# Router of an expert-retrieval layer: query weights as the stationary operand, score matmuls one expert tile later, weight rows of 8 KB

## What is computed

```python
q = (xn @ wq).reshape(B, S, PEER_HEADS, 2, PEER_HALF)          # 8 heads, 2 halves of 128
s1 = einsum('bshd,nd->bshn', q[..., 0, :], k1)                 # 128 keys each
s2 = einsum('bshd,nd->bshn', q[..., 1, :], k2)
t1, i1 = top_k(s1, 16);  t2, i2 = top_k(s2, 16)
top_s, pos = top_k(t1[..., :, None] + t2[..., None, :], 16)    # of 256 candidates
gate = softmax(top_s);  idx = i1 * 128 + i2 at pos             # 16 of 16384 experts
act = gelu(einsum('td,ted->te', x_blk, u[i_blk]))              # rows of 2048 from table u
out = einsum('te,ted->td', g_blk * act, v[i_blk])              # rows of 2048 from table v
```

## Time and profile before

| | |
|---|---|
| median of 3 runs | 3597.04 us (3596.82 to 3602.62) |
| span of the profiled execution | 3600.9 us |
| PE, DVE, POOL, ACT busy | 82%, 51%, 52%, 15% of the span |
| mean granted TensorE clock | 0.907 of full speed |
| HBM read | 1225.74 MB, 341 GB/s over the span |

### The profile page before, as it was taken

The page is one execution under the profiler, slowest core; times in us unless marked ns, Lnnn a source line. Parts: engine busy times, 40 slices in busy tenths (PEclk is TensorE's granted clock), DMA queues, the critical chain, the costliest instruction groups (busy, mean ns, idle before and its releaser), DMA issues.

```text
span 3600.9 us, 28564 instructions
## 1 busy us (share of the span) xinstructions
PE 2935.1 (82%) x8424; PEld 1628.0 (45%) x8424; DVE 1833.3 (51%) x3313; ACT 548.9 (15%) x1123; POOL 1857.2 (52%) x1173
## 2 busy tenths in 40 slices
PE   7999977888878877788779797888888877777777
PEld 6876743444444333333337685444444433333333
DVE  2021145555555566656557833555555555566564
ACT  3344210000000100000023341000000000000001
POOL 4767634444444555555537644454544444545553
PEclk9999989998999888888989898999999988888899
DMA  5544579999998999999975336999999899999998
GB/s 205 175 145 147 179 284 382 376 383 385 375 385 350 420 420 421 420 421 421 420 324 187 105 117 241 377 383 386 385 387 384 363 420 420 421 421 420 420 421 352
DMA packets 240791, 1228.63 MB, mean 341 GB/s; under 512 B 21088, under 2 KB 54624, under 8 KB 108512
## 3 DMA queue, kind: packets, MB, share of 16 engines
q0 software_dynamic: 147456, 1073.81, 72.6%
q1 hardware_dynamic: 92560, 148.67, 12.4%
q10 hardware_dynamic: 720, 5.44, 0.4%
HBM read 1225.74 MB, written 2.10 MB: 341 GB/s over the span
## 4 chain that ended last, share of the span: by engine, by line
PE 29%; DMA 29%; issue 19%; POOL 12%; DVE 9%; ACT 2%; POOLq 0%; DVEq 0%; ACTq 0%; SPq 0%
DMA ring_sb<-in_peer_u_dram,idx_cur 28%; PE bank L908 21%; POOL w_parts L322 8%; PE bank L788 6%; POOL ring_sb L442 3%; DVE ring_sb L1208 2%; POOL ring_sb L433 1%; PE bank L742 1%; DVE arena L1294 1%; DVE arena L1301 1%; ACT diag L606 1%; DVE arena L1302 1%; PE bank L803 0%; DVE shared L1063 0%; DVE shared L1059 0%
## 5 line engine op out<-in xcount | busy, mean ns | idle before, releaser
L908 PE MATMUL bank<-ring_sb,diag 128*128 128x512 f32 x4096 | 1954.6, 640 | 522.9 <-ACT diag L606 522.9
L1208 DVE CUSTOM_DVE_ANT_0 ring_sb<-ring_sb,arena 128x2048 f32<-128x2048 f32 x512 | 1169.4, 2293 | 928.4 <-DMA ring_sb<-in_peer_u_dram,idx_cur 927.8
L908 PEld LDWEIGHTS bank<-ring_sb,diag 128*128 128x128 f32 x4096 | 833.1, 206 | 1635.6 <-issue 1444.4
L442 POOL DMA_INDIRECT ring_sb<-in_peer_v_dram,idx_cur x512 | 690.8, 1349 | 740.2 <-PE bank L908 570.5
L433 POOL DMA_INDIRECT ring_sb<-in_peer_u_dram,idx_cur x512 | 651.8, 1273 | 604.5 <-DVE shared L1208 430.9
L322 POOL TENSOR_TENSOR w_parts<-ring_sb,w_parts 128x2048 fp32r<-128x2048 f32 x98 | 457.9, 4684 | 240.4 <-ACT w_parts L316 240.4
L742 PE MATMUL bank<-w_parts,actT_hi 128*128 128x512 f32 x1664 | 527.8, 399 | 24.9 <-POOL w_parts L322 12.1
L742 PEld LDWEIGHTS bank<-w_parts,actT_hi 128*128 128x128 f32 x1664 | 319.2, 193 | 97.9 <-POOL w_parts L322 15.4
L742 PE MATMUL bank<-w_parts,actT_lo 128*128 128x512 f32 x832 | 330.0, 397 | 0.0
L601 ACT ACTIVATE shared<-shared 128x4 f32<-128x4 f32 (+1 forms) x140 | 28.8, 206 | 1517.2 <-DVE shared L1217 1517.2
L316 ACT CAST w_parts<-ring_sb 128x2048 fp32r<-128x2048 f32 x104 | 198.2, 1910 | 358.3 <-DMA ring_sb<-in_mlstm_w_in_dram 167.3
(11 more groups left out here) (158 smaller groups left out, 1204.1 us busy)
## 6 DMA issues: line engine op xcount, KB each, us to landing
ring_sb<-in_mlstm_w_in_dram SPq DMA_DIRECT2D x48, 1024.0 KB, 5.1
arena<-in_peer_wq_dram SPq DMA_DIRECT2D x28, 1024.0 KB, 11.1
ring_sb<-in_attn_w_in_dram SPq DMA_DIRECT2D x24, 1024.0 KB, 5.2
ring_sb<-in_mlstm_w_out_dram SPq DMA_DIRECT2D x16, 1024.0 KB, 5.1
ring_sb<-in_attn_w_out_dram SPq DMA_DIRECT2D x16, 1024.0 KB, 5.1
ring_sb<-in_peer_u_dram,idx_cur POOLq DMA_INDIRECT x512, 15.3
ring_sb<-in_peer_v_dram,idx_cur POOLq DMA_INDIRECT x512, 14.0
ring_sb<-in_peer_wq_dram SPq DMA_DIRECT2D x4, 1024.0 KB, 8.9
```

The costliest lines, as they stand in the source:

```text
L442: nc.gpsimd.indirect_dma_start(out=v_slot[k % NVS], out_offset=None, in_=v_rows, in_offset=bass.IndirectOffsetOnAxis(ap=idx_cur[par][:, k: ...
L908: last = mm(acc[n][:, :], diag[k % 4][:, :], v_slot[k % NVS][:, n * CH:(n + 1) * CH], start=False, stop=end and k == TOPK - 1, skip_group_ ...
L1208: v.tensor_tensor_reduce(u_slot[k % NU], u_slot[k % NU], xn[b], 1.0, 0.0, ALU.mult, ALU.add, dots[:, k:k + 1]).then_inc(u_used, 1)
```

## The change

Four edits. The query matmuls take a 128 x 128 piece of the query weights as the stationary operand and the tokens as the moving one, so that the result is the transposed query; the transposes, one of the copies and the tile `q_nat` are gone. The router is split in two on PE and ACT: on PE the query matmuls stay ahead of tile 4 and the score matmuls come ahead of tile 5; on ACT the copy of the query comes behind the diagonals of tiles 4 to 7 and the copy of the scores ahead of the third tanh, with the exponentials of the gates (`gate_exp`) behind it. The host lays out the query weights so that a head's 16 pieces are one row of 16 KB per partition, of which each transfer takes 8 KB; before, a row was 1 KB. For the first head and block 1 the score matmuls also come behind the four matmuls of `seed`.

```diff
 # SP
-                    for i in range(2):
-                        sp.dma_start(slots[i], wq[l, i * half:(i + 1) * half, bass.ds(h * (2 * P), 2 * P)]
-                                     .rearrange("(k p) n -> p k n", p=P)).then_inc(landed[i], 16)
+                    for i in range(2):
+                        sp.dma_start(slots[i].rearrange("p k n -> p (k n)"),
+                                     rows[bass.ds(h * P + l * HEADS * P, P), i * SLOT:(i + 1) * SLOT]).then_inc(landed[i], 16)
 # ACT
-                    act.wait_ge(rq_full, n + 1)
-                    nc.scalar.copy(q_nat[:, lo * 2 * P:hi * 2 * P], mis[0][:, lo * 2 * P:hi * 2 * P]).then_inc(rq_out, 1)
-                    act.wait_ge(rt_full, n + 1)
-                    q_t = [t.rearrange("p (s t) -> p s t", s=2)[:, :, lo * P:hi * P] for t in (q_T[:, :], trb[0][:, :])]
-                    nc.scalar.copy(*q_t).then_inc(rt_out, 1)
+                    q_t = [t.rearrange("p (s t) -> p s t", s=2)[:, :, lo * P:hi * P] for t in (q_T[:, :], mis[0][:, :])]
+                    nc.scalar.copy(*q_t).then_inc(rq_out, 1)
+
+                def router_scores(h, blocks=slice(0, NB)):
...
                     for j, (k0, k1) in enumerate(groups):
-                        if j == 1 and head is not None:
-                            router(head)
+                        if j == 2 and head is not None:
+                            router_scores(head)
+                        if j == 2 and more:
+                            gate_exp(gu + 1)
...
-                        if j == 1 and more:
-                            gate_exp(gu + 1)
+                        if j == 1 and head is not None:
+                            router_query(head)
 # PE
-                for b in blocks:
+                t0, t1 = blocks[0] * P, (blocks[-1] + 1) * P
+                for side in range(2):
                     for k in range(KT):
-                        last = mm(mis[0][:, b * 2 * P:(b + 1) * 2 * P], actT[:, k, b * P:(b + 1) * P],
-                                  slots[k // 8][:, k % 8, :], start=(k == 0), stop=(k == KT - 1),
-                                  skip_group_check=True)
+                        last = mm(mis[0][:, side * T + t0:side * T + t1], slots[k // 8][:, k % 8, side * P:(side + 1) * P],
+                                  actT[:, k, t0:t1], start=(k == 0), stop=(k == KT - 1), skip_group_check=True)
                 last.then_inc(rq_full, 1)
+
+            def router_scores(l, h, blocks=(0, 1)):
...
                 pe.wait_ge(rq_out, n + 1)
-                for side in range(2):
-                    for b in blocks:
-                        i = 2 * side + b
-                        last = tp(trb[0][:, i * P:(i + 1) * P],
-                                  q_nat[:, (2 * b + side) * P:(2 * b + side + 1) * P], ident)
-                last.then_inc(rt_full, 1)
-                pe.wait_ge(rt_out, n + 1)
...
                         if k == 4 and head is not None:
                             router(l, head)
+                        if k == 5 and head is not None:
+                            router_scores(l, head)
...
                 router(l, 0, (1,))
                 seed(0)
+                router_scores(l, 0, (1,))
 # host
+            if name == "peer_wq":
+                layers, d, n = a.shape
+                a = a.reshape(layers, d // P, P, n // (2 * P), 2 * P).transpose(0, 3, 2, 1, 4).reshape(layers, n // (2 * P), P, -1)
```

More of the change, by code:

```diff
@@ L98, in trunk_kernel @@
     A_KV = (a_w_in.shape[2] // DH - A_HEADS) // 2
-    HEADS = wq.shape[2] // (2 * P)
+    HEADS = wq.shape[1]
     TOPK = 16
@@ L194, in trunk_kernel @@
         wq0_landed = [sem("wq0_landed0"), sem("wq0_landed1")]
-        rq_full, rq_out, rt_full, rt_out, sc_full, sc_out = (sem(n) for n in ("rq_full", "rq_out", "rt_full", "rt_out", "sc_full", "sc_out"))
+        rq_full, rq_out, sc_full, sc_out = (sem(n) for n in ("rq_full", "rq_out", "sc_full", "sc_out"))
         top_ready, gexp_ready, idx_ready, idx_taken = (sem(n) for n in ("top_ready", "gexp_ready", "idx_ready", "idx_taken"))
@@ L246, in tile @@
             return t.bitcast(dt) if dt is not F32 else t
-        q_nat, q_T, onehot = tile(2 * 2 * P), tile(2 * 2 * P), tile(512)
+        q_T, onehot = tile(2 * 2 * P), tile(512)
         scur, srep, cand, crep = tile(2 * P), tile(2 * P), tile(256), tile(256)
@@ L373, in load_queries @@
                     sp.dma_start(keysT[:, i * P:(i + 1) * P], keys[i][l]).then_inc(keys_in, 16)
-                half = D // 2
+                rows = wq.rearrange("l h p n -> (l h p) n")
                 def load(h, slots=wq_slot, landed=wq_landed):
                     for i in range(2):
-                        sp.dma_start(slots[i], wq[l, i * half:(i + 1) * half, bass.ds(h * (2 * P), 2 * P)]
-                                     .rearrange("(k p) n -> p k n", p=P)).then_inc(landed[i], 16)
+                        sp.dma_start(slots[i].rearrange("p k n -> p (k n)"),
+                                     rows[bass.ds(h * P + l * HEADS * P, P), i * SLOT:(i + 1) * SLOT]).then_inc(landed[i], 16)
                 load(0, wq0_slot, wq0_landed)
@@ L575, in peer, with router_query @@
             def peer(l):
-                def router(h, blocks=slice(0, NB)):
+                def router_query(h, blocks=slice(0, NB)):
                     n = h + (l * (HEADS + 1) + 1) if blocks != slice(0, 1) else l * (HEADS + 1)
@@ L581, in router @@
                     act.wait_ge(rq_full, n + 1)
-                    nc.scalar.copy(q_nat[:, lo * 2 * P:hi * 2 * P], mis[0][:, lo * 2 * P:hi * 2 * P]).then_inc(rq_out, 1)
-                    act.wait_ge(rt_full, n + 1)
-                    q_t = [t.rearrange("p (s t) -> p s t", s=2)[:, :, lo * P:hi * P] for t in (q_T[:, :], trb[0][:, :])]
-                    nc.scalar.copy(*q_t).then_inc(rt_out, 1)
+                    q_t = [t.rearrange("p (s t) -> p s t", s=2)[:, :, lo * P:hi * P] for t in (q_T[:, :], mis[0][:, :])]
+                    nc.scalar.copy(*q_t).then_inc(rq_out, 1)
+                def router_scores(h, blocks=slice(0, NB)):
+                    n = h + (l * (HEADS + 1) + 1) if blocks != slice(0, 1) else l * (HEADS + 1)
+                    lo, hi = blocks.start, blocks.stop
                     act.wait_ge(sc_full, n + 1)
@@ L619, in peer @@
                 copy_groups(name, 0, norm_dst)
-                router(0, slice(0, 1))
+                router_query(0, slice(0, 1))
+                router_scores(0, slice(0, 1))
                 gate_exp(base)
@@ L623, in peer @@
                 copy_groups(name, 1, norm_dst)
-                router(0, slice(1, 2))
+                router_query(0, slice(1, 2))
+                router_scores(0, slice(1, 2))
                 if l == 0:
@@ L776, in router @@
             def router(l, h, blocks=(0, 1)):
-                n = h + (l * (HEADS + 1) + 1) if blocks != (0,) else l * (HEADS + 1)
                 first = isinstance(h, int) and h == 0
@@ L785, in router @@
                         pe.wait_ge(wq_landed[i], h * 16 + l * (HEADS - 1) * 16)
-                for b in blocks:
+                t0, t1 = blocks[0] * P, (blocks[-1] + 1) * P
+                for side in range(2):
                     for k in range(KT):
-                        last = mm(mis[0][:, b * 2 * P:(b + 1) * 2 * P], actT[:, k, b * P:(b + 1) * P],
-                                  slots[k // 8][:, k % 8, :], start=(k == 0), stop=(k == KT - 1),
-                                  skip_group_check=True)
+                        last = mm(mis[0][:, side * T + t0:side * T + t1], slots[k // 8][:, k % 8, side * P:(side + 1) * P],
+                                  actT[:, k, t0:t1], start=(k == 0), stop=(k == KT - 1), skip_group_check=True)
                 last.then_inc(rq_full, 1)
+            def router_scores(l, h, blocks=(0, 1)):
+                n = h + (l * (HEADS + 1) + 1) if blocks != (0,) else l * (HEADS + 1)
                 pe.wait_ge(rq_out, n + 1)
-                for side in range(2):
-                    for b in blocks:
-                        i = 2 * side + b
-                        last = tp(trb[0][:, i * P:(i + 1) * P],
-                                  q_nat[:, (2 * b + side) * P:(2 * b + side + 1) * P], ident)
-                last.then_inc(rt_full, 1)
-                pe.wait_ge(rt_out, n + 1)
                 for b in blocks:
@@ L811, in next_first @@
                 router(l, 0, (0,))
+                router_scores(l, 0, (0,))
             for b in range(NB):
```

## The result

| | before | after |
|---|---|---|
| median, first measurement (6 runs each) | 3602.13 us | 3613.61 us |
| ratio with 95% interval | | 1.0035 (1.0024 to 1.0047) |
| median, second measurement (16 and 8 runs) | 3602.26 us | 3611.05 us |
| ratio with 95% interval | | 1.0028 (1.0017 to 1.0039) |

The change makes the kernel slower by about a third of a per cent: 11.5 us in the first measurement and 8.8 us in the second. The spans of the two profiled executions, 3600.9 and 3620.1, are 19 us apart, but a second profile of the same changed kernel has 3610.5: one span against one span says less here than the medians.

A forecast was written before the change was run, and what follows sets the result against it. Block 0's units were taken as bound by the loop through query, scores, top-k and tile 9's dot product to U(13). +9.4 per-unit and -1.3 first-head us made +8.1: 3600.9 became 3609.0, less 3.9 for the median, 3605.1; range 3590 to 3616.

The forecast's parts named there:

- What bounds the unit: Block 0: gathers restart with U(13), which waits for tile 9's dot product, queued behind the top-k on DVE.
- The term per unit: Block 0, query matmuls' end to U(13): top-k starts 0.67 us later in each of 14 units, +9.4 us.
- The first heads: Block 0's first router: half-wide query matmuls +0.27, copy and transposes -0.90; net -0.63 us per layer, -1.3 in all.
- The rival that loads don't overlap: First head's half-wide query matmuls on PE bound by stationary loads: 12.2 us, +4.1 net per layer, +8.
- The router of the first head for block 1: Block 1's first router ends at about the same time as before; cost 0.
- Nothing for V(12): V(12) issued near 642, 5 us earlier, fills a still full queue; what follows waits for tile 9; worth nothing.
- nothing for the rows: Query weights on SP's queue: 1.5 us saved per unit only lengthens the idle time; cost 0.
- nothing for the lower clock: Tiles 8 to 11 on PE lose up to 3 us in some units, covered for V gathers; cost 0.
- rival of the bytes: Block 0 bound by bytes: shorter weights give -21 us, 3576; with V(12) up to -92, 3505; chance 0.12.
- the mechanism: Later U(13) per unit plus the first head's gain: +8.1 us, range +3 to +15, 3600 to 3612; chance 0.68.
- more expensive case: Low clock on tiles 8 to 11 or load-bound query matmuls: +8 to +42 more, 3613 to 3647; chance 0.10.
- no change: Another 0.7 us of the 5.0 on block 0's path is hidden: 3597; chance 0.10.

The follow-up runs named there:

- run 4: Changed kernel with DVE's top-k behind the dot product of tile 11 instead of tile 8, in block 0 alone; 3487.51 us, ratio 0.9684 to the kernel before.
- run 9: Changed kernel with the top-k behind the dot product of tile 9 instead of tile 8 in block 0; 3538.53 us, ratio 0.9838 to the kernel before.
- run 5: The changed kernel again, unaltered; 3611.05 us, ratio 1.0028 to the kernel before.
- run 1: Changed kernel with the score matmuls back ahead of tile 4 on PE; 3575.04 us, ratio 0.9937 to the kernel before.
- run 2: Kernel before with only the host's 8 KB rows for the query weights; 3599.22 us, ratio 1.0001.
- run 6: Changed kernel with eight filler matmuls on PE ahead of tile 8 in block 0's units; 3610.96 us, ratio 1.0026 to the kernel before.
- run 8: Changed kernel with the top-k behind tile 11 in block 0 and the old 1 KB query-weight rows; 3497.72 us, ratio 0.9713 to the kernel before.
- run 7: Kernel before with the top-k behind tile 11's dot product in block 0; 3551.91 us, ratio 0.9862.
- the first four experiments: One measurement, kernel before 3600.15 us: scores ahead of tile 4 (3575.04), 8 KB rows alone (3599.22), move alone (3635.10), top-k behind tile 11 (3487.51).

## Why the prediction was right

**What bounds the unit** was right: the top-k ahead of tile 9's dot product. Runs 4 and 9 show it by taking it away, whole and in part; run 9 to 4 us of the arithmetic. The row in which U(13)'s wait was put down to PE was a false lead, as read.

**The term per unit** was mis-sized by a little: +0.67 forecast, 17.08 - 16.32 = +0.76 measured. By the rows of PE, ACT and DVE above, the scores start 3.27 us after the query's end (forecast 3.29), ACT's copy 1.20 after that (1.20), and the copy takes 0.59; but from its end at 642.82 to the top-k at 642.98 are 0.16 us, where I took 0.05. This hand-over, put at 0.05 without a row for it, is the whole difference. 14 x 0.76 is 10.6 us. The distance of two U(13), which I named as 93.9, is 95.36 in the unit shown; the twelve such distances inside the two layers average 94.4 in this profile, 93.7 in that of run 5 and 93.0 before, so the forecast lies between the two profiles. Beyond the path, the first profile is longer by 0.26 us per unit in the gathers from U(13) to the next unit and by 0.17 in tiles 0 to 3; in that of run 5 the same two are -0.24 and +0.04. Neither keeps its size from one execution to the other, so I take them as scatter; that they are is not shown.

**The first heads**: forecast -0.63, measured 7.87 - 8.54 = -0.67 in both layers. That it reaches the time was not tried by itself. The half-wide matmuls are not bound by their weight loads: 7.41 us, forecast 7.44. The rival that loads don't overlap is refuted. The router of the first head for block 1, put at the same time as before, took 9.51 us of query matmuls in both layers of the first profile, against 8.95 and 8.83, each time partly at the lower clock. V(4) stands behind it; this term of up to about 1 us per layer is missing in the sum.

**Nothing for V(12), nothing for the rows, nothing for the lower clock**: runs 1, 2 and 6 bear each of them out; run 6 priced half of what the clock costs on tiles 8 to 11. The first two hold only as long as the top-k is in the way: with it behind tile 11 the rows pay (run 8), and the rows of run 7 point to V(12) there. The prediction had this condition in its rival of the bytes. Its price there for the weights, 1.5 x 14 = 21 us, counts two loads too many; twelve units have one, 18 us.

**The sum**: 10.6 - 1.3 = +9.3 us, 0.26%. Both measured intervals, 0.24 to 0.47% and 0.17 to 0.39%, hold it. The forecast was +8.1, or 0.22%: just under the first interval and inside the second. The absolute median of 3613.61 lies 8.5 over the forecast 3605.1, of which 5.1 are the kernel before, measured at 3602.13 beside it and at 3597.04 earlier. So it lies outside the 3600 to 3612 that the mechanism alone gave, and inside the stated range by 2.4 us, thanks to the share of the more expensive case in it. The difference to the kernel beside it, +11.5 and +8.8, is inside the mechanism's own +3 to +15.

**The rivals**: bytes as the bound, no change, and the more expensive cases did not come. Their terms are the ones that the runs priced.

The version to keep is run 4: the change with the top-k behind tile 11 in block 0, 3487.51 us, 3.2% under the kernel before. Without the late top-k the best one is run 1.

## What to carry to other kernels

Where an engine's queue holds a long step that waits for another engine (the top-k here) in front of short steps that release buffers, every other edit is priced by that order. Find the first transfer after the silence and ask what it alone waits for, since work that hides under the silence is free and savings there are worth nothing. The router's edits cost 9 to 11 us with the top-k in place, and their part on PE and ACT gained 54 us with it behind tile 11, so an edit that failed should be tried again when the bound has moved.

## What the hardware showed that I had not expected

The 8 KB rows cut the time of 2.10 MB on SP's queue from 6.5 to 5.0 us. With the DMA engines busy throughout it was 6.3 to 5.0, and 1.07 us of it came back in a regular unit (run 8).

One and the same tile 4 took longer in eleven of 14 units of run 7, at a mean granted clock of 0.68 in the one shown, after PE had waited three times for ACT within 5 us; it moved a V gather by 1.7 us. The issue of a gather takes longer on POOL beside DVE: in the profile of the kernel before, the 293 gathers that start while a dot product runs take 2.20 us (median), the 731 others 0.94; V(12) in the rows of run 7 is such a case.

Executions of one kernel differ by more than the effect in question: the changed kernel's first six runs span 3606.31 to 3621.86 us, and the kernel before spans 3592.48 to 3606.74 us over the 17 runs beside the first four experiments. Inside one profile of the changed kernel the time from the query's end to U(13) stays within 0.3 us over 14 units, while the stretch of gathers from U(13) to the next unit's first tile takes 45.96 to 47.63 us. The same stretch carries most of the difference between the two profiled executions, 3620.1 and 3610.5 us: 46.98 against 46.48 us on average over the 14 units, 7 of the 9.6 us. What makes it longer or shorter was not tried.
